# Rotary embedding of the differential heads: rows swapped on VectorE in place of a turning matmul

## The chip, the cores and the metric

One core of one Trainium2 chip. The metric is the device time of one execution in microseconds (us), as the median of several runs; lower is better.

## The reference, cut to what matters

The program computes two blocks one after the other. The change touches the second one, `second_block`, in each of its two layers (called layer 0 and layer 1 below). There, three kinds of attention are computed from one projection of the input; one of them is differential attention, whose queries and keys are normalized per head and turned by a rotary embedding:

```python
dq = rms_norm_2(dq.reshape(lead + (DIFF_HEADS, 2, DIFF_D)), diff_q_g)   # DIFF_HEADS 4, DIFF_D 64
dk = rms_norm_2(dk.reshape(lead + (DIFF_HEADS, 2, DIFF_D)), diff_k_g)
d_q = apply_rope(d_q, cos_d, sin_d)
d_k = apply_rope(d_k, cos_d, sin_d)

def apply_rope(x, cos, sin):
    x1, x2 = x[..., :half], x[..., half:]        # half = 32
    return jnp.concatenate([x1 * cs - x2 * sn, x2 * cs + x1 * sn], axis=-1)
```

Only the 256 latent tokens are turned, not the 256 context tokens. After it, `diff_attend` takes the softmax of two maps per head and mixes the values with their difference. In layer 1 the context outputs are not needed, so queries exist for the latent tokens alone.

## The kernel before, in words

**Layout.** Features lie on the 128 partitions and tokens along the free axis. Queries and keys of the differential heads are four tiles each of 128 rows (two maps of 64 rows) by 512 tokens; a tile is one of the eight `n` in the code (0 to 3 queries, 4 to 7 keys). The rotary embedding pairs row i of a map with row i+32, so each tile holds four groups of 32 rows (`QUAD`), of which 0 and 1 belong together, and 2 and 3.

**Matmuls and weights.** Each fp32 product is made of three fp32r passes: high part of the weight by high and low part of the input, and low part by high part. Weights come from HBM through a ring of four slots (`load`, L211, on SP's queue), are rounded by ScalarE (`round_weights`, L234, written at L243), and the low part is subtracted by VectorE or GpSimd (`split_weights`, L247, written at L253). Which engine splits which slot is fixed by a plan; the order in which each engine comes to it is written out by hand in its own stream. TensorE waits for `weights_split` before it uses a slot.

**The stage around the change.** `project_heads` (L3272) with `kind == "diff"` runs once in each layer. TensorE makes the eight q and k tiles, then the values, then four gate tiles `z` (L3338, j = 0 to 3). For each q and k tile GpSimd squares (L3232), a matmul sums (L3223), ScalarE takes the root (L3240), and VectorE inverts (L3248, RECIPROCAL) and scales (L3250, which ticks `normed`). When all eight are scaled, VectorE starts the rotary embedding: for each tile a sine product from PSUM (L3265), a cosine product in place (L3266) and the sum (L3269, ticks `roped`). The PSUM operand is the tile with its halves swapped and one of them negated, made by a matmul with the constant matrix `rope_turn` (L3258). Those matmuls stand in TensorE's stream two behind each gate tile: n = 2j and 2j+1 after z tile j. So VectorE's embedding goes at the pace of the gate tiles. After tile n = 4 VectorE splits weight slot z0+4, after the last one slot z0+5, and then it makes the small factors of lambda (L3399 to L3403), for which it waits for ScalarE's exponentials (L3377, after the last gate tile). z0+4 and z0+5 are the first two slots of the next merge, `mix{l}_1`.

**The stage behind it.** `attend_maps` (L4217) interleaves the attention with that merge, a step (three passes, L4162) at a time. TensorE does some steps (3 in layer 0, 6 in layer 1) of the first merge tile, which reads slot z0+4, then the scores of unit 0 (L4270), for which the key of its head must be roped; then 6 steps in layer 0 and 10 in layer 1, of which those past the eighth step of the whole read slot z0+5; then the scores of unit 1, the transposes of unit 0 (L4278), the values (L4289), and so on. VectorE does the maxima (L4375, L4379), splits, and combines the two maps (L4386, L4388, L4390). ScalarE waits for all eight `roped` before it rounds the branch's output (L4208) and does the exponentials (L4338). VectorE's stream is in order, so the maxima of unit 0 stand behind the whole embedding and both splits.

**SP's queue.** At the head of the stage SP loads the cosine and sine table (L3305) and the turning matrix (L3306), and then goes on with the weight stream. GpSimd has, beside the squares, the splits of the slots up to z0+3.

Of the kernel before, what the change touches and what calls it, by code (L numbers as in the profile page):

```python
# [20 lines left out]
P = 128  # L21
# [3 lines left out]
NLAT = 256  # L25
# [45 lines left out]
QUAD = 32  # L71
# [3178 lines left out]
    dve.scalar_tensor_tensor(x, x, gain, r, ALU.mult, ALU.mult).then_inc(b.tick("normed"), 1)  # L3250


def turn_for_rope(b, pe, n, turn, x):
    rows = turn.shape[0]
    pe.wait_ge(b.sem("normed"), b.nth("normed", n + 1))
    if n >= 2:
        pe.wait_ge(b.sem("turned_taken"), b.nth("turned_taken", n - 1))
    pe.matmul(b.psum[0:rows, 6 + n % 2, 0:NLAT], turn, x, start=True, stop=True).then_inc(b.tick("half_turned"), 1)  # L3258


def mix_for_rope(b, dve, n, x, tmp, cos, sin, bank=None):
    rows = x.shape[0]
    t = tmp[0:rows, n % 2, :]
    dve.wait_ge(b.sem("half_turned"), b.nth("half_turned", n + 1))
    dve.tensor_tensor(t, b.psum[0:rows, bank or 6 + n % 2, 0:NLAT], sin, ALU.mult).then_inc(b.tick("turned_taken"), 1)  # L3265
    dve.tensor_tensor(x, x, cos, ALU.mult).then_inc(b.tick("dve_step"), 1)  # L3266
    dve.wait_ge(b.sem("dve_step"), b.all("dve_step"))
    dve.wait_ge(b.sem("turned_taken"), b.nth("turned_taken", n + 1))
    dve.tensor_tensor(x, x, t, ALU.add).then_inc(b.tick("roped"), 1)  # L3269


def project_heads(b, l, kind, seg, m):  # L3272

    d = b.dram
# [3 lines left out]
    with st:  # L3278
        sq = b.sb(st, "head_sq", [P, 2, T])
        rstd = b.sb(st, "head_rstd", [P, 2, T])  # L3280
        if rope:
            tab = b.sb(st, "rope_tab", [P, 2, NLAT])
            turn = b.sb(st, "rope_turn", [P, P])
            tmp = b.sb(st, "rope_tmp", [P, 2, NLAT])
# [8 lines left out]
        def latents(n):  # L3293
            return (m["q"] if n < 4 else m["k"])[:, n % 4, NCTX:T]

        with b.stage() as block:
# [4 lines left out]
            @block.sync  # L3301
            def _(sp):
                if rope:
                    sp.wait_ge(b.sem("scores_ready"), b.nth("scores_ready", 0))
                    sp.dma_start(tab[:], d["c_rope_diff"]).then_inc(b.tick("rope_in", 16), 16)  # L3305
                    sp.dma_start(turn[:], d["c_turn_diff"]).then_inc(b.tick("rope_in", 16), 16)  # L3306
                for x in ("qk", "v", "z"):
                    b.stream(sp, f"{kind}_{x}{l}")

# [7 lines left out]
            @block.tensor  # L3317
            def _(pe):
                for n in range(8):
                    if n == 4 and not rope and not joint:  # L3320
                        pe.wait_ge(b.sem("input_split"), b.nth("input_split", 0))
                    if rope and b.banks[qt + n][0] == 0:
                        pe.wait_ge(b.sem("gated"), b.nth("gated", 0))
                    if joint and n == 4:
                        pairs = b.passes(q0 + n, slice(0, P), b.input(ALL))
                        pe.wait_ge(*b.weights_split(q0 + n))
                        for k in range(KD):
                            pe.wait_ge(b.sem("input_split"), b.nth("input_split", k + 1 - KD))
                            b.product(pe, qt + n, lambda x: x, pairs[3 * k:3 * k + 3], first=k == 0, last=k == KD - 1, frees=False)
                    elif rope or n >= FIRST:  # L3330
                        b.products(pe, f"{kind}_qk{l}", n, cols[n], b.input(cols[n]))
                    if n >= lag:
                        sum_for_norm(b, pe, n - lag, b.half_ones[:], sq, cols[n - lag])
                for s in range(VS):
                    b.products_by_token(pe, f"{kind}_v{l}", s, b.tokens)
                    if s < lag:
                        sum_for_norm(b, pe, 8 - lag + s, b.half_ones[:], sq, cols[8 - lag + s])
                for j in range(4):  # L3338
                    b.products(pe, f"{kind}_z{l}", j, seg, b.input(seg))
                    if rope:  # L3340
                        if j == 0:
                            pe.wait_ge(b.sem("rope_in"), b.nth("rope_in", 32))
                            pe.wait_ge(b.sem("lam_products"), b.nth("lam_products", 1))
                            pe.wait_ge(b.sem("deviation_ready"), b.nth("deviation_ready", 8))
                            pe.matmul(b.psum[:, 4, 0:2], b.ones[0:64, :], prod[:], start=True, stop=True)\
                                .then_inc(b.tick("lam_sums"), 1)
                        for n in (2 * j, 2 * j + 1):
                            turn_for_rope(b, pe, n, turn[:], latents(n))

            @block.scalar  # L3350
            def _(act):
# [28 lines left out]
            def _(dve):  # L3380
# [6 lines left out]
                for n in range(8):  # L3387
                    scale_for_norm(b, dve, n, tile(n), rstd, P, cols[n], column(b, gains[n // 4], l))
                if rope:
                    dve.wait_ge(b.sem("rope_in"), b.nth("rope_in", 32))  # L3390
                    for n in range(8):
                        mix_for_rope(b, dve, n, latents(n), tmp, tab[:, 0, :], tab[:, 1, :])
                        if n == 4:
                            b.split_weights(dve, "dve", z0 + 4)
                    b.split_weights(dve, "dve", z0 + 5)
# [2 lines left out]
                    x = b.lam[:, l]  # L3398
# [1355 lines left out]
```

## Time and profile before

| what | value |
|---|---|
| median of 3 runs | 2382.57 us (2380.94 to 2384.29) |
| span of the profiled execution | 2377.0 us |
| TensorE (PE) busy | 2311.8 us, 97% |
| VectorE (DVE) busy | 1570.0 us, 66% |
| ScalarE (ACT) busy | 1216.2 us, 51% |
| GpSimd (POOL) busy | 420.5 us, 18% |
| mean granted TensorE clock | 0.993 of full speed |

The profile is of one execution. Its own time is known as its span, from the first to the last instruction; the median of the timed runs is 5.6 us above that span, which holds what lies around it and the difference between executions. Busy shares are averages over stages with different limits. An "idle before" in brackets is the time that an engine stood still before an instruction and what released it. A matmul's record is longer than its pace where the next one overlaps it, so paces are read from starts.

### The profile page before, as it was taken

The numbers are of one execution on the slowest core, as the hardware profiler recorded it, in microseconds if no ns is written. First come the engines' busy times: TensorE is split into PE (matmuls) and PEld (weight loads), VectorE is DVE, ScalarE is ACT, GpSimd is POOL, SyncE is SP. The second block draws the span as 40 slices with busy tenths as digits, with TensorE's granted clock in tenths as the row PEclk, the third lists the DMA queues.
The fourth block names the chain that finished last, engine by engine and source line by source line (L and its number), as shares of the span: only waits on it lengthen the run. The fifth ranks groups of instructions, "written<-read, shape, count | busy, mean of one in ns | idle before, by whom it ended". The sixth has DMA issues, their size and how long they took to land. (4 is left out here: it accounts for less than half of the span.)

```text
span 2377.0 us, 35065 instructions
## 1 busy us (share of the span) xinstructions
PE 2311.8 (97%) x13734; PEld 1914.8 (81%) x13734; DVE 1570.0 (66%) x2386; ACT 1216.2 (51%) x2095; POOL 420.5 (18%) x272
## 2 busy tenths in 40 slices
PE   8998999999999999999999999999999999999999
PEld 5776788887889888799998767777767888778888
DVE  5967979778766666687676464643576465574685
ACT  3656545223328434567454355764366243576374
POOL 0000000000006444000002431004201126303301
PEclk9999999999999999999999999999999999999999
DMA  9734427666545332356664231223222333334344
GB/s 327 234 103 159 152 81 216 183 197 182 153 131 140 91 89 81 113 157 183 190 184 116 78 92 56 63 54 86 71 71 70 99 89 108 108 89 122 89 124 134
DMA packets 419340, 301.01 MB, mean 127 GB/s; under 512 B 13443, under 2 KB 389353, under 8 KB 419177
## 3 DMA queue, kind: packets, MB, share of 16 engines
q1 hardware_dynamic: 418064, 298.33, 43.5%
q8 instruction: 110, 1.80, 0.3%
q10 hardware_dynamic: 1112, 0.44, 0.1%
q14 instruction: 54, 0.43, 0.1%
HBM read 297.68 MB, written 1.05 MB: 126 GB/s over the span
## 5 line engine op out<-in xcount | busy, mean ns | idle before, releaser
L243 ACT ACTIVATE weights_hi<-wslots 128x1024 fp32r<-128x1024 f32 (+1 forms) x408 | 425.6, 1047 | 215.8 <-PE psum L306 180.1
L306 PE MATMUL psum<-input_hi,weights_hi 128*128 128x512 f32 (+1 forms) x1376 | 486.7, 354 | 1.5 <-PEq L1281 0.6
L306 PE MATMUL psum<-input_hi,weights_lo 128*128 128x512 f32 (+1 forms) x1376 | 474.9, 345 | 0.0
L306 PE MATMUL psum<-input_lo,weights_hi 128*128 128x512 f32 (+1 forms) x1376 | 474.6, 345 | 0.0
L253 DVE TENSOR_TENSOR weights_lo<-wslots,weights_hi 128x1024 fp32r<-128x1024 f32 x277 | 338.7, 1233 | 117.5 <-ACT weights_hi L243 116.7
L253 POOL TENSOR_TENSOR weights_lo<-wslots,weights_hi 128x1024 fp32r<-128x1024 f32 (+1 forms) x128 | 306.2, 2402 | 576.7 <-ACT weights_hi L243 576.1
L306 PEld LDWEIGHTS psum<-input_hi,weights_hi 128*128 128x128 f32 x1376 | 258.9, 188 | 42.9 <-issue 6.8
L306 PEld LDWEIGHTS psum<-input_lo,weights_hi 128*128 128x128 f32 x1376 | 259.1, 188 | 33.8 <-issue 2.6
L306 PEld LDWEIGHTS psum<-input_hi,weights_lo 128*128 128x128 f32 x1376 | 258.7, 188 | 33.0
L306 PE MATMUL psum<-ffn_hidden_hi,weights_hi 128*128 128x512 f32 (+1 forms) x512 | 172.3, 336 | 0.0
L306 PE MATMUL psum<-ffn_hidden_hi,weights_lo 128*128 128x512 f32 (+1 forms) x512 | 170.8, 334 | 0.0
L306 PE MATMUL psum<-ffn_hidden_lo,weights_hi 128*128 128x512 f32 (+1 forms) x512 | 170.7, 333 | 0.0
L3248 DVE RECIPROCAL head_rstd<-head_rstd 128x512 f32<-128x512 f32 (+1 forms) x32 | 94.4, 2951 | 88.3 <-ACT head_rstd L3240 88.3
L4162 PE MATMUL psum<-input_hi,weights_hi 128*128 128x512 f32 (+1 forms) x384 | 133.3, 347 | 0.3 <-ACT att_o L4180 0.3
L4162 PE MATMUL psum<-input_hi,weights_lo 128*128 128x512 f32 (+1 forms) x384 | 128.5, 335 | 0.0
L4162 PE MATMUL psum<-input_lo,weights_hi 128*128 128x512 f32 (+1 forms) x384 | 128.3, 334 | 0.0
L306 PEld LDWEIGHTS psum<-ffn_hidden_hi,weights_hi 128*128 128x128 f32 x512 | 96.1, 188 | 13.0 <-issue 3.4
L306 PEld LDWEIGHTS psum<-ffn_hidden_hi,weights_lo 128*128 128x128 f32 x512 | 96.4, 188 | 10.2
L306 PEld LDWEIGHTS psum<-ffn_hidden_lo,weights_hi 128*128 128x128 f32 x512 | 96.2, 188 | 9.8
L1657 ACT ACTIVATE ffn_hidden<-psum 128x512 f32<-128x512 f32 (+1 forms) x64 | 31.4, 491 | 118.2 <-PE psum L306 112.5
L2703 DVE SCALAR_TENSOR_TENSOR ssd_conv<-psum,cols,ssd_conv 128x508 f32<-128x508 f32 (+3 forms) x128 | 87.3, 682 | 4.5
L4162 PEld LDWEIGHTS psum<-input_hi,weights_hi 128*128 128x128 f32 x384 | 72.5, 189 | 11.8 <-issue 4.4
(605 smaller groups left out, 4880.6 us busy)
## 6 DMA issues: line engine op xcount, KB each, us to landing
wslots<-w_in SPq DMA_DIRECT2D x130, 512.0 KB, 4.0
wslots<-ffn_w SPq DMA_DIRECT2D x128, 512.0 KB, 4.7
wslots<-ssd_w_in SPq DMA_DIRECT2D x49, 512.0 KB, 4.0
wslots<-ada_w SPq DMA_DIRECT2D x32, 512.0 KB, 4.7
h<-w_ada SPq DMA_DIRECT2D x28, 512.0 KB, 4.3
wslots<-gla_w_in SPq DMA_DIRECT2D x24, 512.0 KB, 4.9
input_raw<-ada_w SPq DMA_DIRECT2D x24, 512.0 KB, 4.1
ada_slab<-ada_w SPq DMA_DIRECT2D x24, 512.0 KB, 3.9
```

The source lines that it names most:

```text
L243: act.activation(self.high(self.whi_r, n), self.slot(n), ACT.Copy)\
L253: engine.tensor_tensor(self.low(n), self.slot(n), self.high(self.whi, n), ALU.subtract)\
L306: ins = pe.matmul(out_of(self.bank(g)), l, r, start=first and i == 0, stop=last and i == len(pairs) - 1, skip_group_check=not (first and l ...
L1657: act.activation(hid[:, j % NH, :], b.bank(g)[:, a:e], ACT.Relu).then_inc(b.reads_out(g), 1)
L2703: ins = dve.scalar_tensor_tensor(dst[:, :, o], src[:, :, i], tap(k), dst[:, :, o], ALU.mult, ALU.add)
L3248: dve.reciprocal(r, r).then_inc(b.tick("dve_step"), 1)
L4162: ins = pe.matmul(b.bank(g)[:, a:e], w, u, start=x == 0, stop=x == len(pairs) - 1, skip_group_check=True)
```

## The change: what it does

The turning matmuls, TensorE's waits for them and the load of the turning matrix go. VectorE writes the sine products of 32 rows straight to the 32 rows of the other half, one product with the sign turned, so a tile takes four products of 32 rows in place of one of 128. TensorE's and VectorE's waits for the loaded tables count one load instead of two. VectorE now waits for its own products (`turned_taken`) before the cosine product overwrites the tile, and before the first tile for all eight `normed`. The place in VectorE's stream, the two splits in it and all that follows are the same.

```diff
-def turn_for_rope(b, pe, n, turn, x):
-    rows = turn.shape[0]
-    pe.wait_ge(b.sem("normed"), b.nth("normed", n + 1))
+def rope_for_heads(b, dve, n, x, tmp, cos, sin):
+
+    t = tmp[:, n % 2, :]
+    if n == 0:
+        dve.wait_ge(b.sem("normed"), b.nth("normed", 8))
     if n >= 2:
-        pe.wait_ge(b.sem("turned_taken"), b.nth("turned_taken", n - 1))
-    pe.matmul(b.psum[0:rows, 6 + n % 2, 0:NLAT], turn, x, start=True, stop=True).then_inc(b.tick("half_turned"), 1)
-
-
-def mix_for_rope(b, dve, n, x, tmp, cos, sin, bank=None):
-    rows = x.shape[0]
-    t = tmp[0:rows, n % 2, :]
-    dve.wait_ge(b.sem("half_turned"), b.nth("half_turned", n + 1))
-    dve.tensor_tensor(t, b.psum[0:rows, bank or 6 + n % 2, 0:NLAT], sin, ALU.mult).then_inc(b.tick("turned_taken"), 1)
+        dve.wait_ge(b.sem("roped"), b.nth("roped", n - 1))
+    for o in range(0, P, 2 * QUAD):
+        u, v = slice(o, o + QUAD), slice(o + QUAD, o + 2 * QUAD)
+        dve.tensor_tensor(t[v, :], x[u, :], sin[u, :], ALU.mult)
+        ins = dve.scalar_tensor_tensor(t[u, :], x[v, :], -1.0, sin[v, :], ALU.mult, ALU.mult)
+    ins.then_inc(b.tick("turned_taken"), 1)
+    dve.wait_ge(b.sem("turned_taken"), b.nth("turned_taken", n + 1))
     dve.tensor_tensor(x, x, cos, ALU.mult).then_inc(b.tick("dve_step"), 1)
     dve.wait_ge(b.sem("dve_step"), b.all("dve_step"))
-    dve.wait_ge(b.sem("turned_taken"), b.nth("turned_taken", n + 1))
     dve.tensor_tensor(x, x, t, ALU.add).then_inc(b.tick("roped"), 1)
...
-                    sp.dma_start(turn[:], d["c_turn_diff"]).then_inc(b.tick("rope_in", 16), 16)
...
-                            pe.wait_ge(b.sem("rope_in"), b.nth("rope_in", 32))
+                            pe.wait_ge(b.sem("rope_in"), b.nth("rope_in", 16))
...
-                        for n in (2 * j, 2 * j + 1):
-                            turn_for_rope(b, pe, n, turn[:], latents(n))
...
-                    dve.wait_ge(b.sem("rope_in"), b.nth("rope_in", 32))
+                    dve.wait_ge(b.sem("rope_in"), b.nth("rope_in", 16))
                     for n in range(8):
-                        mix_for_rope(b, dve, n, latents(n), tmp, tab[:, 0, :], tab[:, 1, :])
+                        rope_for_heads(b, dve, n, latents(n), tmp, tab[:, 0, :], tab[:, 1, :])
                         if n == 4:
                             b.split_weights(dve, "dve", z0 + 4)
```

## Rows read from the trace of the kernel before

**Rows 1.** The page's chain that ended last, shares of the span by engine.
```profile
PE 40%; DVE 3%; ACT 2%; POOL 1%; issue 1%; DMA 0%; DVEq 0%; SPq 0%; ACTq 0%
```

**Rows 2.** The chain in order of time, layer 1: start us, us, what.
```profile
2255.29 2.12 PE psum L4162 x18
...
2258.46 3.62 PE psum L4162 x30
...
2262.08 1.11 PE psum L4270 x4
2263.19 1.27 DVE small L4375 x2
...
2269.53 1.62 PE psum L4289 x8
...
2277.03 0.89 PE psum L4289 x8
```

**Rows 3.** PE's timeline around a pair of turning matmuls, layer 0: start us, us.
```profile
1706.87 0.39 PE L306 MATMUL psum<-input_hi,weights_lo 128*128 128x512 f32 x1
1707.10 1.02 PE L3258 MATMUL psum<-att_qk,rope_turn 128*128 128x256 f32 x4
...
1708.42 0.40 PE L306 MATMUL psum<-input_hi,weights_lo 128*128 128x512 f32 x1
```

**Rows 4.** DVE's timeline, layer 1: last scaling, tile n = 5, second split, first maxima.
```profile
2233.42 2.91 DVE L3250 SCALAR_TENSOR_TENSOR att_qk<-att_qk,cols,head_rstd 128x512 f32<-128x512 f32 x1
...
2252.43 1.22 DVE L253 TENSOR_TENSOR weights_lo<-wslots,weights_hi 128x1024 fp32r<-128x1024 f32 x1
2253.56 0.42 DVE L3265 TENSOR_TENSOR rope_tmp<-psum,rope_tab 128x256 f32<-128x256 f32 x1
2253.90 0.41 DVE L3266 TENSOR_TENSOR att_qk<-att_qk,rope_tab 128x256 f32<-128x256 f32 x1
2254.35 0.43 DVE L3269 TENSOR_TENSOR att_qk<-att_qk,rope_tmp 128x256 f32<-128x256 f32 x1
...
2257.16 1.22 DVE L253 TENSOR_TENSOR weights_lo<-wslots,weights_hi 128x1024 fp32r<-128x1024 f32 x1
...
2258.61 1.28 DVE L4375 TENSOR_REDUCE small<-psum 128x1 f32<-128x512 f32 x2
```

**Rows 5.** DVE's timeline, earlier stages: instructions on 32 rows, other rows and same rows.
```profile
770.19 0.34 DVE L2680 TENSOR_SCALAR ssd_state<-ssd_state 32x256 f32<-32x256 f32 x1
770.54 0.34 DVE L2681 TENSOR_SCALAR ssd_state<-ssd_state 32x256 f32<-32x256 f32 x1
...
1472.51 0.23 DVE L3633 TENSOR_SCALAR mla_movers<-ident,cols 32x32 f32<-32x32 f32 x1
1472.66 0.23 DVE L3634 TENSOR_SCALAR mla_movers<-mla_turn,cols 32x32 f32<-32x32 f32 x1
```

**Rows 6.** DVE's groups by form: busy us, mean ns | idle before.
```profile
L3193 DVE SCALAR_TENSOR_TENSOR input_lo<-in_raw,mod,input_hi 128x256 fp32r<-128x256 f32 x16 | 7.7, 480 | 0.4 <-ACT input_hi L3179 0.4
```

**Rows 7.** POOL's timeline: last but one split of the stage in layer 0, last two in layer 1.
```profile
1690.69 2.67 POOL L253 TENSOR_TENSOR weights_lo<-wslots,weights_hi 128x1024 fp32r<-128x1024 f32 x1
...
2235.93 2.66 POOL L253 TENSOR_TENSOR weights_lo<-wslots,weights_hi 128x1024 fp32r<-128x1024 f32 x1
...
2241.85 2.38 POOL L253 TENSOR_TENSOR weights_lo<-wslots,weights_hi 128x1024 fp32r<-128x1024 f32 x1 [3.26 <-ACT weights_hi L243]
```

**Rows 8.** Timeline of all engines at the end of the stage, layer 0.
```profile
1721.91 0.17 ACT L3377 ACTIVATE lam<-psum 128x2 f32<-128x2 f32 x1
...
1722.91 1.13 PE L4270 MATMUL psum<-att_qk 64*128 64x512 f32 x4
...
1724.15 0.68 DVE L4375 TENSOR_REDUCE small<-psum 128x1 f32<-128x512 f32 x1
```

**Rows 9.** Busy time by stretch, layer 1: us, busy us by engine, PEclk, DMA, GB/s.
```profile
2264.00:2266.00 2.00, 0.12 (x1) 0.15 (x2) 2.00 (x5) 1.44 (x5) 0.00 (x0) 1.00 0.00 0
...
2268.00:2270.00 2.00, 1.71 (x10) 1.59 (x9) 2.00 (x6) 2.00 (x4) 0.00 (x0) 0.50 1.09 306
```

## The prediction, made before the change was run

> **What bounds the kernel now.** The chain that ended last comes first: PE 40%, DVE 3% [rows 1], so a microsecond taken off PE counts where PE is what everyone waits for. The change sits in two short stretches, one in each layer, so the chain in order of time is read there [rows 2]. In layer 1 it runs through PE up to the scores of unit 1 at 2262.08, and at 2263.19 it passes to DVE. Then DVE's timeline is read for how near it is to PE before that. The second split starts at 2257.16 right behind the last rope sum, and the maxima of unit 0 start at 2258.61 [rows 4], while PE ended the scores they read at 2258.46 [rows 2]. DVE comes to them 0.15 us later than PE. The two engines reach the attention side by side, so what DVE does later here, the layer does later. In layer 0 it is the same to 0.1 us: scores end at 1722.91 + 1.13 = 1724.04, maxima start at 1724.15 [rows 8].
>
> **What PE loses.** Eight turning matmuls a layer, in four pairs. Around one pair, the passes start at 1706.87 and, three passes on, at 1708.42: 1.55 us, where the plain pace in this stretch is 0.23 us a pass (1706.87 to 1707.10), so 0.69. A pair costs 0.86 us [rows 3], four pairs 3.5 us a layer. There is no stall of PE in it, since each pair's input was scaled long ago. SP issues one load less a layer, ahead of a weight stream that waits for free slots: nothing; the work of splitting hides it.
>
> **What DVE gains and loses.** Before, its pace was set by PE: the last scaling ended at 2233.42 + 2.91 = 2236.33, the last sum at 2257.16 [rows 4]. Now it may start at 2236.33 in layer 1, and in layer 0 at the same point of the stage, but the work is larger.
> - Per tile. A product of 128 x 256 takes 0.42 us, its successor starting 0.34 later (2253.56 to 2253.90), or 0.45 later where it waits for the one before (2253.90 to 2254.35) [rows 4]. One with a scalar takes 0.48 [rows 6]. No row has the new form, which reads 32 rows and writes 32 others. Fewer rows do not shorten an instruction of this kind in any row that I read, so I keep 0.42 and 0.48. For the spacing there are two rows: a pair of 32-row instructions on different rows (L2680 has rows 0 to 31, L2681 rows 32 to 63) start 0.35 apart at a duration of 0.34, while a pair on the same rows starts 0.15 apart at a duration of 0.23 [rows 5]. The new products change their rows each time, so they are nearest to the first pair: no overlap. That gives 0.43 + 0.49 + 0.43 + 0.52 (the wait for them in it) + 0.45 (cosine) + 0.43 (sum, followed by other rows) = 2.75 us a tile, 22.0 us for eight. Bounds: with overlap 0.34 + 0.40 + 0.34 + 0.51 + 0.45 + 0.34 = 2.38, 19.0 us; with a wait's spacing everywhere 2.9, 23.2 us.
> - GpSimd. The last scaling, 128 x 512, took 2.91 us, where a split of twice the elements takes 1.22 [rows 4]; it ended 0.4 behind the start of GpSimd's last split but one, 2235.93, and that split took 2.66 where the next takes 2.38 [rows 7]. So a DVE instruction with two SBUF inputs and a GpSimd split exclude each other. The new products have two SBUF inputs (the old sine product had one in PSUM) and start where GpSimd still splits. The last but one ends at 2238.59; a product that waits has its start-up behind it (0.2, my estimate from the same 0.4), so the embedding effectively starts at 2238.4. The last one, at 2241.85 for 2.38, holds DVE another 2.2, less what it shares with the product in flight [rows 7]. In layer 0 the split of 1690.69 gives 1693.2 [rows 7], and the last one follows at the same distance. Bounds of the two together: 0, and 4.4 plus GpSimd's 0.3.
> - Layer 1, the sum. Five tiles: 2238.4 + 2.2 + 13.75 = 2254.35. The split of z0+4 (1.13, spacing 2252.43 to 2253.56 [rows 4]) ends it at 2255.5; three tiles more, 2263.75. The old time was 2257.16: DVE is 6.6 us later for the split of z0+5 and for all behind it. PE, now free of its pairs, could begin the merge at 2255.29 - 3.5 = 2251.8 and waits for z0+4 until 2255.5. It does 8 steps and the scores of unit 0, and waits for z0+5 until 2264.9. Then come 8 steps at 3.62 / 10 us each [rows 2], 2.9 us, and the scores of unit 1, 1.1: 2268.9. DVE, which took 2258.61 to 2263.19 for its work up to the maxima of unit 1, is there at 2269.8. PE's saving of layer 1 is gone, and the layer is 6.6 us longer. Nothing after that takes it back: from 2270 on PE is the chain, as late as it was released.
> - PE's clock. Before, PE did 0.12 us of work in 2264 to 2266, and in 2268 to 2270 it had 0.50, which is 1.2 GHz [rows 9]; the values of a unit took 1.62 us there and 0.89 at full clock [rows 2]. Now two more stretches without work, 3.7 and some 5 us, stand ahead. Their half clock falls mostly in time in which PE waits for DVE anyway. I take 0.8 us for what does not; bounds 0 and 3.4.
> - Layer 0, the sum. 1693.2 + 2.2 + 22.0 + 2 x 1.13 = 1719.7. ScalarE's exponentials move with the gate tiles to 1722.1 - 3.5 = 1718.6, so lambda's factors (0.3) end at 1720.0; the scores end at 1724.04 - 3.5 = 1720.5 [rows 8]. DVE is in time by 0.5, and the layer keeps 3.5 us. In this layer the cover is the longer gate tiles (512 tokens instead of 256), and it is thin.
>
> A rule speaks for the change. The Trainium skill, Vector Engine (DVE) Microarchitecture Reference, section 3.8, says that cross-quadrant moves (from one group of 32 partitions to another) by a 32-partition op are free. Taken as overlap like any other, that is the lower bound above. The skill's VectorE: DVE Perf Modes, "Two Vector instructions with no wait between them", says in turn that an instruction is held until all earlier ones have finished where the first row group of its input or output differs from the last one used; the spacing of 0.35 at a duration of 0.34 agrees with this, in one pair [rows 5].
>
> **Total.** -3.5 + 6.6 + 0.8 = +3.9 us against the profiled span of 2377.0, so 2380.9 for that; the median of the runs is 5.6 above that span, and the same 3.9 on it gives 2386.5. A measurement of this kernel can tell 0.2% (4.8 us) from no change; 3.9 is inside.
>
> **The rivals.**
> - *Rows crossed with overlap.* DVE's paces stay 0.34, three microseconds less in layer 1: -3.5 + 3.6 = about 0, 2382.7. For it: DVE's ordinary overlap [rows 4]. Against: the 0.35 [rows 5]. Chance 0.11.
> - *GpSimd in the way only once or not at all.* The 2.2 or both parts go: layer 1 +2.4 to +4.4, total -1 to +1, 2382.5. Against: the 2.91 us [rows 4]. Chance 0.06.
> - *DVE covered in both layers.* PE keeps all 7.0 us: 2375.6. It needs the embedding of layer 1 done by 2253.7, that is, under 2.05 us a tile with no hold by GpSimd; only if 32 rows were much cheaper than 128. Chance 0.05.
> - *The clock decides: slower.* After the standstill ahead of z0+5 PE works at 1.2 GHz when DVE needs it. The 8 steps (2.9) and the scores (1.1) double: ready at 2272 or later instead of 2268.9, against DVE's 2269.8. From 0.9 us of lost work on, every lost microsecond is the kernel's. That gives +2.5 in place of 0.8, 2388.2, and up to 2390 where the later units too start at half clock, as the values did. For it: 0.50 soon after only 2 us of standstill [rows 9]. Against: before that there was a full pace again within some us [rows 2], and a drop that was there already may only move. Chance 0.30.
> - The forecast itself: 0.48. Of this, 0.08 lies above 4.8 us, since a tile at 2.9 adds 1.2 in layer 1 and up to 0.7 in layer 0.
>
> **How the numbers follow.** Faster by over 0.2%: the covered case, 0.05. Slower by over 0.2%: 0.30 + 0.08 = 0.38. Within: 0.40 + 0.11 + 0.06 = 0.57. The predicted time is that of the likeliest case, 2386.5. The range, 2379.5 to 2390.5, holds the first two rivals with both bounds of GpSimd's price and the slow clock; it leaves out the covered case and the sum of all upper bounds.
>
> **What would show it.** Right: in layer 1 the last rope sum ends near 2263.8 and the split of z0+5 starts there; a first product waits for GpSimd until about 2238.6 and one is over 2 us long near 2242; products of 32 rows start 0.43 to 0.49 apart; PE idles before L4162 twice, released by DVE's L253. In layer 0 the last sum ends near 1718.6, the maxima start near 1720.6, released by PE. Wrong: products 0.34 apart; no long one at 2242; DVE idle before the maxima in layer 1; a layer 0 whose maxima follow lambda's factors without idle time.

## The result, and the profile after

| | before | after |
|---|---|---|
| median | 2381.28 us, 20 runs (2375.91 to 2384.29) | 2386.63 us, 20 runs (2382.01 to 2390.43) |
| ratio | | 1.0021, 95% interval 1.0015 to 1.0027 |
| span of the profiled execution | 2377.0 us | 2385.3 us (its own time: 2387.55 us) |
| TensorE busy | 2311.8 us, 97% | 2314.1 us, 97% |
| VectorE busy | 1570.0 us, 66% | 1600.4 us, 67% |
| mean granted clock, profiled execution | 0.993 | 0.988 |
| mean granted clock, timed executions | 0.9915 (34 runs, with the first experiments) | 0.9893 (20 runs) |

The change costs 5.0 us (3.6 to 6.4). The 0.2% that the forecast called no change is 4.8 us, which lies inside this interval, so the measurement doesn't tell on which side of it the change falls. The median of before fell by 1.3 us with more runs, so the forecast's difference, +3.9, is what to compare, not its 2386.5. Differences in this text are the ratio less 1, by 2381 us. They can lie up to 1.3 us from the difference of two medians (here 5.35).

The spans of the two profiles differ by 8.3 us, and most of that isn't the change's. The last scaling of layer 0, the last VectorE instruction ahead of the new code, starts 5.2 us later already. Of the two fences, the first is from the kernel before, the second from the one after (VectorE's timeline in layer 0: start us, us, then engine, line, operation, tiles, and idle before in brackets):

```profile
1688.18 2.92 DVE L3250 SCALAR_TENSOR_TENSOR att_qk<-att_qk,cols,head_rstd 128x512 f32<-128x512 f32 x1
```

```profile
1693.35 2.92 DVE L3250 SCALAR_TENSOR_TENSOR att_qk<-att_qk,cols,head_rstd 128x512 f32<-128x512 f32 x1
...
1722.83 1.22 DVE L253 TENSOR_TENSOR weights_lo<-wslots,weights_hi 128x1024 fp32r<-128x1024 f32 x1
...
1724.83 0.15 DVE L3399 TENSOR_SCALAR lam<-lam 128x1 f32<-128x1 f32 x1
1726.53 1.29 DVE L4371 TENSOR_REDUCE small<-psum 128x1 f32<-128x512 f32 x2 [1.54 <-PE psum L4266]
```

So the change is read by distances. From the start of this scaling to the maxima of unit 0 it took 1724.15 - 1688.18 = 35.97 us before ([rows 8] has the 1724.15) and takes 1726.53 - 1693.35 = 33.18 now: layer 0 gains 2.79 us, and its maxima wait 1.54 us for TensorE, so VectorE isn't the bound there. It isn't 3.5 because TensorE meets a wait that the last pair of turning matmuls had covered. The chain of the kernel after, layer 0 (start us, us, what):

```profile
1705.88 16.56 PE psum L306 x72
...
1722.46 0.61 ACT att_o L3369
...
1723.11 2.33 PE psum L4158 x9
1725.44 1.06 PE psum L4266 x4
```

The merge's first tile needs the bank (a part of PSUM) of the last gate tile, and ScalarE has to evacuate that first: 0.7 us between the last L306 and the first L4158.

Layer 1, VectorE's timeline after, to be held against [rows 4]:

```profile
2236.54 2.91 DVE L3250 SCALAR_TENSOR_TENSOR att_qk<-att_qk,cols,head_rstd 128x512 f32<-128x512 f32 x1
2239.55 2.44 DVE L3262 TENSOR_TENSOR rope_tmp<-att_qk,rope_tab 32x256 f32<-32x256 f32 x1
...
2245.09 2.57 DVE L3262 TENSOR_TENSOR rope_tmp<-att_qk,rope_tab 32x256 f32<-32x256 f32 x1
...
2249.04 0.41 DVE L3262 TENSOR_TENSOR rope_tmp<-att_qk,rope_tab 32x256 f32<-32x256 f32 x1
2249.47 0.41 DVE L3263 SCALAR_TENSOR_TENSOR rope_tmp<-att_qk,rope_tab 32x256 f32<-32x256 f32 x1
2249.90 0.42 DVE L3262 TENSOR_TENSOR rope_tmp<-att_qk,rope_tab 32x256 f32<-32x256 f32 x1
...
2250.78 0.43 DVE L3266 TENSOR_TENSOR att_qk<-att_qk,rope_tab 128x256 f32<-128x256 f32 x1
...
2251.70 0.41 DVE L3262 TENSOR_TENSOR rope_tmp<-att_qk,rope_tab 32x256 f32<-32x256 f32 x1
...
2256.90 1.22 DVE L253 TENSOR_TENSOR weights_lo<-wslots,weights_hi 128x1024 fp32r<-128x1024 f32 x1
...
2266.00 1.22 DVE L253 TENSOR_TENSOR weights_lo<-wslots,weights_hi 128x1024 fp32r<-128x1024 f32 x1
...
2267.46 0.68 DVE L4371 TENSOR_REDUCE small<-psum 128x1 f32<-128x512 f32 x1
```

A tile takes 2251.70 - 2249.04 = 2.66 us, the products start 0.43 apart, and two products are over 2 us long. GpSimd's last two splits of the stage end within 0.3 us of those two (GpSimd's timeline, kernel after; to be held against [rows 7]): 2241.72 against 2241.99, 2247.38 against 2247.66.

```profile
2239.06 2.66 POOL L253 TENSOR_TENSOR weights_lo<-wslots,weights_hi 128x1024 fp32r<-128x1024 f32 x1 [0.15 <-ACT weights_hi L243]
2244.98 2.40 POOL L253 TENSOR_TENSOR weights_lo<-wslots,weights_hi 128x1024 fp32r<-128x1024 f32 x1 [3.27 <-ACT weights_hi L243]
```

From the scaling to the maxima it takes 2267.46 - 2236.54 = 30.92 us, where it took 2258.61 - 2233.42 = 25.19 before [rows 4]: 5.73 us longer.

The two layers are +2.9 us of the 8.3 between the spans. Another 5.2 lie ahead of the change, as said. The stretch between the layers, from the maxima of unit 0 in layer 0 to the last scaling in layer 1, takes 0.7 more (510.01 us against 509.27), and the rest of the kernel behind the maxima of layer 1 takes 0.55 less (117.84 against 118.39).

TensorE's waits in layer 1 between 2243 and 2280 say what it waits for (what waits <- for whom: us in total, times, longest us):

```profile
PE psum L4158 <- DVE weights_lo L253: 6.7, 2, 3.4
```

VectorE enters the chain with it. The page's shares were PE 40% and DVE 3% [rows 1]; after:

```profile
PE 39%; DVE 4%; ACT 2%; POOL 1%; issue 1%; DMA 0%; DVEq 0%; SPq 0%; ACTq 0%
```

And the clock behind the two waits (busy time by stretch, kernel after; third figure from the end PEclk). In 2260 to 2262 and 2270 to 2272 it is near the 1.2 GHz level; before, three stretches in a row showed 0.88, 0.50 and 0.77 (the middle one is in [rows 9]).

```profile
2258.00:2260.00 2.00, 1.73 (x8) 1.76 (x9) 1.89 (x6) 0.00 (x0) 0.00 (x0) 0.58 0.27 44
2260.00:2262.00 2.00, 2.00 (x12) 1.96 (x10) 1.91 (x5) 0.00 (x0) 0.00 (x0) 0.57 0.73 218
2268.00:2270.00 2.00, 2.00 (x14) 2.00 (x13) 2.00 (x5) 1.17 (x3) 0.00 (x0) 0.64 0.78 227
2270.00:2272.00 2.00, 2.00 (x11) 1.78 (x12) 1.53 (x4) 1.23 (x3) 0.00 (x0) 0.51 0.10 35
```

The half clock behind the second wait makes VectorE wait in turn. The chain of the kernel after (start us, us, what), and VectorE's maxima of unit 1, first after, then before:

```profile
2267.37 4.50 PE psum L4158 x24
2271.87 1.18 PE psum L4266 x4
```

```profile
2273.02 1.29 DVE L4371 TENSOR_REDUCE small<-psum 128x1 f32<-128x512 f32 x2 [1.17 <-PE psum L4266]
```

```profile
2263.17 1.29 DVE L4375 TENSOR_REDUCE small<-psum 128x1 f32<-128x512 f32 x2 [0.17 <-PE psum L4270]
```

The maxima of unit 1 start 5.56 us behind those of unit 0, where it was 4.56.

### The profile page after: what moved, and what is told of

Its sections match the earlier page's. It is cut to its first block and busy times, and to the rows that moved or that the text cites. A ratio compares the mean times of both kernels' runs of the same rounds, so it can differ in the third digit from the quotient of the medians.

```text
span 2385.3 us, 35019 instructions
## 1 busy us (share of the span) xinstructions
PE 2314.1 (97%) x13702; PEld 1917.6 (80%) x13702; DVE 1600.4 (67%) x2434; ACT 1216.1 (51%) x2095; POOL 420.1 (18%) x272
## 5 line engine op out<-in xcount | busy, mean ns | idle before, releaser
L306 PE MATMUL psum<-input_hi,weights_hi 128*128 128x512 f32 (+1 forms) x1376 | 485.8, 353 | 1.5 <-PEq L1281 0.6
L306 PE MATMUL psum<-input_hi,weights_lo 128*128 128x512 f32 (+1 forms) x1376 | 475.3, 345 | 0.0
L306 PE MATMUL psum<-input_lo,weights_hi 128*128 128x512 f32 (+1 forms) x1376 | 474.9, 345 | 0.0
L306 PEld LDWEIGHTS psum<-input_hi,weights_hi 128*128 128x128 f32 x1376 | 259.1, 188 | 42.9 <-issue 6.8
L306 PEld LDWEIGHTS psum<-input_lo,weights_hi 128*128 128x128 f32 x1376 | 259.1, 188 | 33.8 <-issue 2.6
L306 PEld LDWEIGHTS psum<-input_hi,weights_lo 128*128 128x128 f32 x1376 | 258.8, 188 | 33.0
L306 PE MATMUL psum<-ffn_hidden_hi,weights_hi 128*128 128x512 f32 (+1 forms) x512 | 172.3, 336 | 0.0
L306 PE MATMUL psum<-ffn_hidden_hi,weights_lo 128*128 128x512 f32 (+1 forms) x512 | 170.8, 334 | 0.0
L306 PE MATMUL psum<-ffn_hidden_lo,weights_hi 128*128 128x512 f32 (+1 forms) x512 | 170.7, 333 | 0.0
L4158 PE MATMUL psum<-input_hi,weights_hi 128*128 128x512 f32 (+1 forms) x384 | 135.6, 353 | 7.6 <-DVE weights_lo L253 6.7
L4158 PE MATMUL psum<-input_hi,weights_lo 128*128 128x512 f32 (+1 forms) x384 | 130.4, 339 | 0.0
L4158 PE MATMUL psum<-input_lo,weights_hi 128*128 128x512 f32 (+1 forms) x384 | 130.3, 339 | 0.0
L306 PEld LDWEIGHTS psum<-ffn_hidden_hi,weights_hi 128*128 128x128 f32 x512 | 96.1, 188 | 13.1 <-issue 3.4
L306 PEld LDWEIGHTS psum<-ffn_hidden_hi,weights_lo 128*128 128x128 f32 x512 | 96.4, 188 | 10.1
L306 PEld LDWEIGHTS psum<-ffn_hidden_lo,weights_hi 128*128 128x128 f32 x512 | 96.2, 188 | 9.7
L4158 PEld LDWEIGHTS psum<-input_hi,weights_hi 128*128 128x128 f32 x384 | 74.4, 194 | 19.8 <-issue 11.4
```

The lines of the kernel that those rows point to most:

```text
L306: ins = pe.matmul(out_of(self.bank(g)), l, r, start=first and i == 0, stop=last and i == len(pairs) - 1, skip_group_check=not (first and l ...
L4158: ins = pe.matmul(b.bank(g)[:, a:e], w, u, start=x == 0, stop=x == len(pairs) - 1, skip_group_check=True)
```

## The experiments

The theory: layer 0 keeps TensorE's saving, layer 1 loses more by a later end of VectorE's in-order stream. Inside that stand three disputed prices: rows that change with every product, the exclusion by GpSimd, and the clock. All kernels are changes of the kernel after; the ratios are to the kernel before, timed on the same chip. The distances (last scaling to maxima of unit 0) are from each kernel's one profile.

### One layer at a time

Each kernel has the new embedding in one layer and the turning matmuls, their load and `mix_for_rope` in the other. Shown is the first kernel; the second has `(1,)` for `(0,)`.

```
+    swap = l in (0,)
...
+                        if not swap:
+                            for n in (2 * j, 2 * j + 1):
+                                turn_for_rope(b, pe, n, turn[:], latents(n))
...
-                        rope_for_heads(b, dve, n, latents(n), tmp, tab[:, 0, :], tab[:, 1, :])
+                        (rope_for_heads if swap else mix_for_rope)(b, dve, n, latents(n), tmp, tab[:, 0, :], tab[:, 1, :])
```

> The new rope in layer 0 alone, the old one with its turning matmuls in layer 1. Theory A (VectorE is late in layer 1 only, because its tiles are not covered there): layer 0 keeps what its profile shows, 3.5 us of TensorE less a new wait of 0.7 for ScalarE's evacuation, so 2.8 us faster than before (ratio 0.9988), and in its trace the last rope sum of layer 0 ends before ScalarE's exponential for lambda. Theory B (the loss lies in both layers or is one of the clock, wherever it falls): 2 us or more slower, ratio 1.001.

> The new rope in layer 1 alone. Theory A: all of the loss and none of the gain: VectorE's maxima of unit 0 come about 5.7 us later, the kernel is 5.3 us slower than before (ratio 1.0022), or up to 8 if half-clock stretches add to it. Theory B: about half of what both layers together gave, 2.7 us slower.

Layer 0 alone: 2376.85 us, ratio 0.9985 (0.9974 to 0.9995), so -3.6 us; distances 33.18 and 25.20. Layer 1 alone: 2387.82 us, 1.0032 (1.0021 to 1.0044), +7.6 us; distances 35.97 and 30.93. The layers' distances are independent: each is that of the kernel before or after to 0.01 us. In time, -3.6 + 7.6 = +4.0 stands against +5.0 for both, with intervals of 2 us and more to either side.

### Without the sine part

Each tile's four sine products and the sum are left out, and only the cosine product stays.

```
-    for o in range(0, P, 2 * QUAD):
-        u, v = slice(o, o + QUAD), slice(o + QUAD, o + 2 * QUAD)
-        dve.tensor_tensor(t[v, :], x[u, :], sin[u, :], ALU.mult)
-        ins = dve.scalar_tensor_tensor(t[u, :], x[v, :], -1.0, sin[v, :], ALU.mult, ALU.mult)
...
+    dve.tensor_tensor(x, x, cos, ALU.mult).then_inc(b.tick("roped"), 1)
```

> Leaves out the four sine products and the sum of every tile in both layers, so VectorE has one product a tile. Theory A: with VectorE out of the way TensorE keeps what the turning matmuls cost, 2.8 us in layer 0 and some 3.5 in layer 1: 6.3 us faster than before, ratio 0.9974, and no wait of TensorE for VectorE's splits. Rival C (something else is next in layer 1, ScalarE's evacuation or the weights): 3 us faster or less, 0.9988.

2373.28 us, 0.9969 (0.9958 to 0.9980), -7.4 us. Layer 0's distance is 33.18, the same as with the whole embedding: there VectorE costs nothing, and 2.79 us is all that TensorE's freed time gives. Layer 1's distance is 21.42, 3.77 under the kernel before, and now the maxima wait for TensorE (VectorE's timeline, layer 1):

```profile
2253.48 1.29 DVE L4360 TENSOR_REDUCE small<-psum 128x1 f32<-128x512 f32 x2 [0.78 <-PE psum L4255]
```

So with VectorE out of the way the distances fall by 2.79 + 3.77 = 6.6 us. This is the ceiling for the kernels below.

### GpSimd's last split given to VectorE

```
-        feature_major(f"diff_z{l}", w[:, z0 + 2 * BW:z0 + 3 * BW], narrow=range(4) if own else ())
+        feature_major(f"diff_z{l}", w[:, z0 + 2 * BW:z0 + 3 * BW], low=["pool"] * 3 + ["dve"], narrow=range(4) if own else ())
...
                         rope_for_heads(b, dve, n, latents(n), tmp, tab[:, 0, :], tab[:, 1, :])
+                        if n == 0:
+                            b.split_weights(dve, "dve", z0 + 3)
```

> The last weight split of GpSimd in this stage (slot z0+3) goes to VectorE, behind its first tile, in both layers. Theory A with the exclusion of GpSimd and VectorE: the long sine product of the second tile (2.57 us) is back at 0.42, VectorE pays 1.14 for the split instead of 2.15 for the hold, so the maxima of unit 0 in layer 1 come 1.0 us earlier and the kernel is 1.0 us faster than the change, 4.3 slower than before (1.0018). Rival D (the long product is not GpSimd's doing): it stays long, and the kernel is 1.1 us slower than the change.

2384.38 us, 1.0014 (1.0002 to 1.0025); distances 33.19 and 30.73. VectorE's timeline in layer 1: the product that was 2.57 us long, the third of the second tile, is 0.42.

```profile
2231.85 2.91 DVE L3250 SCALAR_TENSOR_TENSOR att_qk<-att_qk,cols,head_rstd 128x512 f32<-128x512 f32 x1
2234.86 2.44 DVE L3262 TENSOR_TENSOR rope_tmp<-att_qk,rope_tab 32x256 f32<-32x256 f32 x1
...
2240.24 1.23 DVE L253 TENSOR_TENSOR weights_lo<-wslots,weights_hi 128x1024 fp32r<-128x1024 f32 x1 [0.73 <-ACT weights_hi L243]
...
2242.35 0.42 DVE L3262 TENSOR_TENSOR rope_tmp<-att_qk,rope_tab 32x256 f32<-32x256 f32 x1
```

The long product goes with GpSimd's split; the one ahead, whose split stays, is still 2.44. That shows who held it; for the one ahead it is inferred, from its end beside the end of GpSimd's split. Expected were 1.0 us, and the distance falls by 0.2, since the split (1.23) and its wait for ScalarE's rounding (0.73) now stand in VectorE's stream.

### Both VectorE splits earlier

```
-                        if n == 4:
+                        if n == 2:
                             b.split_weights(dve, "dve", z0 + 4)
-                    b.split_weights(dve, "dve", z0 + 5)
+                        if n == 4:
+                            b.split_weights(dve, "dve", z0 + 5)
```

> The change with VectorE's splits moved forward: slot z0+4 behind tile 2, z0+5 behind tile 4, so TensorE finds its weights, while VectorE's stream is as long as before. Theory A (the end of VectorE's stream sets layer 1): the maxima of unit 0 come at the same distance (30.9 us behind the start of the last scaling), TensorE's 6.7 us of waits for the splits only move to the transposes of unit 0, and the kernel gains at most the 1.2 us that the maxima of unit 1 waited: 1.0016 of before, mean clock as with the change, 0.989. Rival E (the waits for the splits themselves are the price): 4 us or more off the change, 1.0004 of before or below, mean clock back at 0.9915.

2386.31 us, 1.0019 (1.0010 to 1.0028); distances 33.19 and 30.92, the same as the change to 0.01 us. TensorE's two waits for splits are gone, and others stand in their place (TensorE's waits, layer 1):

```profile
PE psum L4267 <- ACT prob L4335: 6.7, 1, 6.7
PE psum L4267 <- DVE att_qk L3268: 1.4, 1, 1.4
```

Whether TensorE works or waits while VectorE is at the embedding doesn't move the maxima of unit 0. They stand at the end of VectorE's stream, and that end didn't move.

### Products on the same rows in pairs

Two tiles go together, so that two products on the same rows follow each other.

```
+        for i in range(2):
+            dve.tensor_tensor(tmp[v, i, :], xs[i][u, :], sin[u, :], ALU.mult)
+        for i in range(2):
+            ins = dve.scalar_tensor_tensor(tmp[u, i, :], xs[i][v, :], -1.0, sin[v, :], ALU.mult, ALU.mult)
...
```

The cosine products and the sums of the two tiles follow each other likewise.

> The same products, but two tiles at a time: each product of the second tile follows the one of the first on the same rows. Theory F (an instruction waits for the end of the one before it where its rows differ from that one's): the second of each pair starts 0.34 us behind the first instead of 0.43, four times a pair of tiles, and cosine and sum lose two waits of 0.12: 0.6 us a pair of tiles, 2.4 us a layer, the maxima of unit 0 in layer 1 at 28.5 instead of 30.9, the kernel 1.0011 of before. Rival G (crossing rows costs 0.43 in itself, whatever went before): products stay 0.43 apart, only the two waits go, 1 us a layer.

2381.08 us, 1.0005 (0.9996 to 1.0014); distances 33.19 and 28.76. VectorE's timeline in layer 1, each line two instructions, and the maxima of unit 0:

```profile
2244.42 0.75 DVE L3262 TENSOR_TENSOR rope_tmp<-att_qk,rope_tab 32x256 f32<-32x256 f32 x2
2245.18 0.75 DVE L3264 SCALAR_TENSOR_TENSOR rope_tmp<-att_qk,rope_tab 32x256 f32<-32x256 f32 x2
2245.94 0.75 DVE L3262 TENSOR_TENSOR rope_tmp<-att_qk,rope_tab 32x256 f32<-32x256 f32 x2
...
2261.23 1.29 DVE L4374 TENSOR_REDUCE small<-psum 128x1 f32<-128x512 f32 x2 [0.24 <-PE psum L4269]
```

A pair takes 0.76 where two products took 0.86: with a duration of 0.42 the second starts 0.34 behind the first, as ordinary products do [rows 4]. So a change of rows costs 0.09 us. The pairs give back 2.2 us of the 5.7, and VectorE is earlier by 2.4, since the maxima now wait 0.24 for TensorE: 16 pairs by 0.10 are 1.6, and the rest comes from the cosine products and the sums.

### Four tiles to an instruction

```
+        dve.tensor_tensor(tmp[v], x[u], sin[u].broadcast_to([QUAD, 4, NLAT]), ALU.mult)
+        ins = dve.scalar_tensor_tensor(tmp[u], x[v], -1.0, sin[v].broadcast_to([QUAD, 4, NLAT]), ALU.mult, ALU.mult)
...
```

with `x` the four query or the four key tiles, and a weight split behind each group.

> Four tiles in one instruction (1024 elements a row instead of 256), six instructions for the queries and six for the keys. Theory A with a fixed part per instruction: 1.22 us for four times the elements instead of four times 0.43, 7.4 us for four tiles, 14.8 for eight instead of 21.3. The maxima of unit 0 in layer 1 at 24.4 behind the last scaling (before: 25.2), so layer 1 gains 0.8 and layer 0 its 2.9: ratio 0.9985 of before, mean clock 0.9915. Rival H (the loss has another source than the length of VectorE's stream): no faster than before.

2379.74 us, 0.9994 (0.9984 to 1.0003); distances 33.18 and 24.68. VectorE's timeline in layer 1:

```profile
2238.15 3.31 DVE L3261 TENSOR_TENSOR rope_tmp<-att_qk,rope_tab 32x1024 f32<-32x1024 f32 x1
2241.47 1.21 DVE L3262 SCALAR_TENSOR_TENSOR rope_tmp<-att_qk,rope_tab 32x1024 f32<-32x1024 f32 x1
...
2243.93 3.32 DVE L3262 SCALAR_TENSOR_TENSOR rope_tmp<-att_qk,rope_tab 32x1024 f32<-32x1024 f32 x1
```

1.22 us for four tiles against 4 x 0.43 = 1.72. Layer 1 is back to where it was before the change, 0.5 us under it, with two products 2.1 us too long, beside GpSimd's last two splits, still in it. The time fell less than the distances, by 1.4 us (3.8 less to 0.7 more) where 0.9985, 3.6 us, was expected.

### Query tiles in VectorE's idle time

VectorE stands still in this stage until ScalarE has the roots. Here each query tile is embedded behind the next tile's scaling, and the key tiles go by four at the end, with both splits behind them.

```
                     scale_for_norm(b, dve, n, tile(n), rstd, P, cols[n], column(b, gains[n // 4], l))
+                    if rope and 1 <= n <= 4:
...
+                        rope_for_heads(b, dve, n - 1, latents(n - 1), tmp, tab[:, 0, :], tab[:, 1, :])
                 if rope:
...
+                    rope_for_four(b, dve, 1, m["k"][:, :, NCTX:T], tmp[:], tab, True)
+                    b.split_weights(dve, "dve", z0 + 4)
                     b.split_weights(dve, "dve", z0 + 5)
```

> A version meant to beat both: the four query tiles are roped one by one behind the scaling of tiles 1 to 4, in the 1.0 to 2.9 us in which VectorE waits for the next root, and the four key tiles at the end in wide instructions. Theory A: VectorE ends 12 us behind the last scaling, TensorE decides in both layers, as with the kernel without sine products: 6.2 us faster than before, ratio 0.9974. Rival I (the late scaling of the keys delays ScalarE, and with it TensorE's banks or the last scaling by 3 us or more): ratio 0.9985 or above.

2374.93 us, 0.9971 (0.9960 to 0.9982): 6.9 us under the kernel before (6.2 by the medians), and so under both kernels of this study. The last scaling itself moves here, so the distance is taken from the first reciprocal of the stage: 2256.12 - 2195.17 = 60.95 us, the same as without the sine part (2253.48 - 2192.53 = 60.95), where the kernel before has 64.72. VectorE's timeline in layer 1:

```profile
2249.98 2.35 DVE L253 TENSOR_TENSOR weights_lo<-wslots,weights_hi 128x1024 fp32r<-128x1024 f32 x2
2254.93 0.16 DVE L3412 TENSOR_TENSOR lam<-lam 128x1 f32<-128x1 f32 x1 [2.60 <-ACT lam L3389]
...
2256.12 1.29 DVE L4388 TENSOR_REDUCE small<-psum 128x1 f32<-128x512 f32 x2 [0.78 <-PE psum L4283]
```

VectorE now waits for ScalarE (2.60) and for TensorE (0.78). From the first reciprocal to the last scaling it takes 2238.55 - 2195.17 = 43.38 us, against 2233.42 - 2193.89 = 39.53 before: four tiles of 2.66, 10.6 us of work, made the stage's front only 3.9 us longer. The distances are 2.79 and 3.77 us under those of the kernel before: the ceiling of 6.6 us is reached, and the change pays in both layers.

### TensorE's two new waits filled

TensorE does twelve products more ahead of each of its two waits for splits in layer 1. Beside this kernel the kernel after was timed once more.

```
+            if (l, r, p) == (1, 1, 0) and i < 2:
+                for _ in range(12):
+                    pe.matmul(b.psum[:, 7, :], b.UH_r[:, 0, 0:P], b.UH_r[:, 0, 0:512], start=True, stop=True)
             pe.wait_ge(*b.weights_split(n))
```

> The changed kernel with 12 more products (128x512, 0.23 us apart at full clock, 2.8 us together) ahead of each of TensorE's two new waits in layer 1 (3.4 and 3.3 us in the profile of the changed kernel). Their results are read by nobody. They end before the wait does, so the work that counts starts no later. Theory, the standstills themselves bring the half clock behind them: the merge's products then run at full clock (0.12 us apart instead of 0.21 behind the first wait), the mean clock of the executions goes from 0.989 back towards the 0.9915 of the kernel before, and the time falls by 2 to 5 us, to a ratio of 1.000 to 1.0015. Rival, the lower mean clock has another cause, or what it costs lies in TensorE's waiting anyway: the same as the changed kernel, 1.002. Second rival, more work brings the drop sooner: 1.003 or more.

> The changed kernel once more, unchanged, beside the one before and the one with TensorE's waits filled. Theory: +5 us again, 1.0015 to 1.003, with a mean clock about 0.002 below that of the kernel before. Rival, the difference in clock was the luck of those executions: 1.0005 to 1.001, clocks equal.

The kernel after again: 2387.18 us, 1.0021 (1.0012 to 1.0029), mean clock over its executions 0.9892 against 0.9916 before. Filled: 2387.21 us, 1.0026 (1.0016 to 1.0035), mean clock 0.9896. The filling kept the clock up behind the first wait only. TensorE's timeline behind the first filled wait has the merge at full clock (PEclk 1.00 from 2254 to 2262, where the kernel after had 0.58 and 0.57); behind the second it starts so, 0.12 us a pass, and falls after some eight passes:

```profile
2251.45 2.91 PE L4152 MATMUL psum<-input_hi 128*128 128x512 f32 x12
2254.95 0.39 PE L4161 MATMUL psum<-input_hi,weights_hi 128*128 128x256 f32 x1 [0.59 <-DVE weights_lo L253]
...
2259.06 2.91 PE L4152 MATMUL psum<-input_hi 128*128 128x512 f32 x12
2264.07 0.39 PE L4161 MATMUL psum<-input_hi,weights_hi 128*128 128x256 f32 x1 [2.09 <-DVE weights_lo L253]
...
2264.86 0.28 PE L4161 MATMUL psum<-input_hi,weights_hi 128*128 128x256 f32 x1
2264.98 0.31 PE L4161 MATMUL psum<-input_lo,weights_hi 128*128 128x256 f32 x1
2265.09 0.41 PE L4161 MATMUL psum<-input_hi,weights_lo 128*128 128x256 f32 x1
```

But the distance of layer 1 is 30.93, as before the filling, and the time is that of the change. The lost clock behind the first wait lay in time in which TensorE waits for VectorE anyway. Behind the second the filling did not keep the clock up (2.09 us of that wait stayed empty, since TensorE came to it earlier), so for that half the experiment is inconclusive: VectorE waits 1.11 us for the scores of unit 1 here too.

The second profile of the kernel after has a half-clock stretch more. VectorE's maxima of units 1 and 2 in layer 1, and a stretch ahead of the latter:

```profile
2271.54 1.29 DVE L4371 TENSOR_REDUCE small<-psum 128x1 f32<-128x512 f32 x2 [1.15 <-PE psum L4266]
...
2277.76 1.29 DVE L4371 TENSOR_REDUCE small<-psum 128x1 f32<-128x512 f32 x2 [1.04 <-PE psum L4266]
```

```profile
2274.00:2276.00 2.00, 1.75 (x8) 1.56 (x10) 1.93 (x5) 1.98 (x4) 0.00 (x0) 0.51 0.28 38
```

## Why the prediction was right, and what it missed

The kernel went as forecast in kind and nearly in size: a gain in layer 0, a larger loss in layer 1, +3.9 us forecast and +5.0 (3.6 to 6.4) measured, 2386.5 against 2386.63. The last agreement is luck: the base was 1.3 us lower than the median that the forecast started from, and the cost higher. There is luck in the sum too: -3.5 + 6.6 = +3.1 for the two layers is near the +2.9 that their distances give, with 0.7 us too much on the gain and 0.9 too much on the loss. And +5.0 lies at the border of 0.2%, with 0.57 of the forecast's chances inside and 0.38 on slower. The distances of all profiles, beside the times (us against the kernel before; "both" adds the two layers, "timed" is the ratio less 1 by 2381):

| kernel | layer 0 | layer 1 | both | timed | mean clock, timed executions |
|---|---|---|---|---|---|
| after | -2.79 | +5.73 | +2.9 | +5.0 | 0.9893 |
| after, again | -2.79 | +5.73 | +2.9 | +5.0 | 0.9892 |
| layer 0 alone | -2.79 | +0.01 | -2.8 | -3.6 | 0.9918 |
| layer 1 alone | 0.00 | +5.74 | +5.7 | +7.6 | 0.9901 |
| no sine part | -2.79 | -3.77 | -6.6 | -7.4 | 0.9923 |
| VectorE splits z0+3 | -2.78 | +5.54 | +2.8 | +3.3 | 0.9898 |
| splits earlier | -2.78 | +5.73 | +2.9 | +4.5 | 0.9886 |
| rows in pairs | -2.78 | +3.57 | +0.8 | +1.2 | 0.9905 |
| four tiles | -2.79 | -0.51 | -3.3 | -1.4 | 0.9904 |
| waits filled | -2.79 | +5.74 | +2.9 | +6.2 | 0.9896 |
| queries early | -2.79 | -3.77 | -6.6 | -6.9 | 0.9911 |

- **TensorE's saving, 3.5 us a layer.** The pairs were priced rightly, but layer 0 keeps 2.8. The step that failed is "no stall of PE in it": there was none before, and the removal made one, 0.7 us for ScalarE's evacuation of the last gate tile. In layer 1 the kernel without the sine part gains 3.8: the four pairs, of which the first takes 1.06 us in the chain of the kernel before, and the 0.15 by which VectorE was late.
- **Fewer rows don't shorten a product, and rows that change don't overlap.** Right: 0.41 to 0.42 us each, 0.43 apart. The pairs on the same rows give 0.34, the same as [rows 4]. The rule that the Trainium skill gives in VectorE: DVE Perf Modes, "Two Vector instructions with no wait between them", that an instruction is held where its first row group differs, is what these runs show. The "free" of section 3.8 of its Vector Engine (DVE) Microarchitecture Reference did not hold here, if it is read as overlap: the kernel pays 0.09 us for each change and a full duration for each 32 rows. Crossing adds nothing to the duration itself, 0.41 to 0.42 us against the 0.42 of 128 rows [rows 4].
- **A tile of 2.75 us.** It takes 2.66. The over-sized term is the product with a scalar, 0.48 from [rows 6]; here it takes 0.41 to 0.42. Eight tiles make 0.7 us, and with small differences elsewhere the second split starts 29.46 us behind the last scaling, where 2263.75 - 2233.42 = 30.33 was forecast. So the shift is 5.7, not 6.6.
- **GpSimd in the way twice.** Right, in place and size: 2.44 and 2.57 us long, and the second goes with the split.
- **Layer 0 covered.** Right: the maxima wait for PE by 1.54 us; the slack was forecast as 0.5 and is larger mainly by the evacuation's 0.7.
- **The clock, 0.8 us.** This is the term that was mis-sized, if the rest is to be charged to it: the two distances sum to +2.9 us, and +5.0 was measured, twice.
  - *What the profiles show of it in layer 1.* The clock rival's mechanism is there. Behind the standstill ahead of z0+5 the eight steps and the scores take 4.50 + 1.18 = 5.7 us, where the forecast has 4.0. VectorE waits 1.17 us for them, and unit 1 comes 1.0 us later, not 2.5. What follows differs between the two profiles of the changed kernel. In the first, the half clock of the kernel before at the transposes and values of unit 0 [rows 2] is gone (PEclk 1.00 from 2272 on), and from the maxima of unit 0 to the end it takes 0.5 us less than before: as the prediction had it against this rival, the drop moved. In the second, VectorE waits another 1.04 us at unit 2, and that stretch takes 0.5 us more (118.90 against 118.39).
  - *Where the rest lies.* From the last scaling of layer 0 to the end the two profiles are 3.1 and 4.2 us longer than that of the kernel before. Of this, 0.7 lies between the layers in both (510.01 and 509.99 us against 509.27), but the kernel with layer 0 alone has 509.18 there and the one without the sine part 509.85, so it isn't tied to the change. The remainder of the measured 5.0 would lie ahead of the change, in code that is the same. One or two profiles of a kernel can't settle that: in the eleven profiles of kernels with the same code up to the last scaling of layer 0 (all but queries early), this scaling starts anywhere between 1688.15 and 1693.35, that of the kernel before at 1688.18.
  - *That it goes with the clock.* Among the timed executions whose mean clock was 0.990, the changed kernel takes 2385.2 us (mean of 10) and the kernel before 2382.1 (mean of 11); at 0.991 it is 2383.4 (3) against 2381.5 (35). At an equal clock they are 2 to 3 us apart, about as far as the distances say, and the other 2 us go with the lower clock. This is a connection, not a cause. The stretches below full clock in layer 1 explain a part of it at most: in the profile after they are worth 1.7 us of lost clock more than before, 0.0007 of the mean, where the timed executions fell by 0.0022.
  - *What standstill does for it.* Four kernels in which TensorE stands still for 5.7 us or more in layer 1, or does the filling products in this time (after, layer 1 alone, splits earlier, waits filled), have 1.6 to 3.3 us more than their distances, and mean clocks 0.0014 to 0.0030 below the kernel before. Five others (layer 0 alone, no sine part, VectorE splits z0+3, rows in pairs, queries early) are within 0.8 us. It isn't a clean line: of these five, VectorE splitting z0+3 leaves TensorE standing as long (6.5 us) and rows in pairs for 4.2 us, while four tiles to an instruction has 3.1 us of it and 1.9 us of excess. Each single interval is 2 us or more to either side, so only the kernel after, timed twice (3.6 to 6.4 and 2.9 to 6.9), is above its distances beyond the noise. Filling brought nothing, but it held the clock behind one wait only. Why the changed kernel gets a lower clock stays open.
- **The rivals.** Overlap in spite of crossed rows: out, by the 0.43. GpSimd once or not at all: out. Covered in both layers: out for this kernel, but the order with the queries early makes it come true. Its condition was named as an embedding done by 2253.7; with the queries early the last sum ends at 2250.07, and the kernel is 6.9 us faster than before where the rival had 7.0. The totals of the first two rivals leave out the 0.8 us for the clock that the forecast has.

## What to carry to other kernels

Work taken from the busiest engine is worth its time only where the engine that takes it over ends in time, so ask for each stage what stands last in that engine's in-order stream and when it ends; here the same edit gave 2.8 us in one layer and cost 5.7 in the other. VectorE pays here by the instruction and its free size, not by its rows (32x256 and 128x256 both 0.41 to 0.43 us, 32x1024 and 128x1024 both 1.21 to 1.23): put tiles side by side in the free dimension, put instructions on the same rows one after the other (0.09 us each), and put them where the engine waits anyway. Before removing work from a stream, look for what it covered at its end.

## What was not expected of the hardware

- A SCALAR_TENSOR_TENSOR with the constant -1.0 as its scalar takes 0.41 to 0.42 us on 32x256 fp32, no more than a plain TENSOR_TENSOR; the one of [rows 6], 128x256 with a scalar from a tile and an fp32r output, takes 0.48.
- A change of rows costs 0.09 us and no more: 0.43 apart against 0.34, at a duration of 0.42.
- Distances within the two stretches repeat to 0.01 us from kernel to kernel, while the same code ahead of them ends up to 5 us apart. To judge a change of 0.2% in a profile, measure between two instructions around it and not by the span.
- The mean granted clock differs between kernels by more than its scatter (0.9893 in 20 executions and 0.9892 in 11 against 0.9915 in 34 of the kernel before; single ones 0.988 to 0.991 against 0.990 to 0.994), though TensorE's work is nearly the same.
